# Sparse attention on one core: in each round TensorE turns the last unit's probabilities before it takes the values of the unit three rounds back

## What is computed

```python
s = jnp.einsum('bqgrd,bngd->bgrqn', qb, kc)                    # compressed
p_cmp = jnp.where(vis, jax.nn.softmax(jnp.where(vis, s, NEG)), 0.0)
o_cmp = jnp.einsum('bgrqn,bngd->bqgrd', p_cmp, vc)
...
p_slc = jax.nn.softmax(s, axis=-1)                             # selected
o_slc = jnp.einsum('bgrqkl,bgqkld->bqgrd', p_slc, vg)
...
p_win = jax.nn.softmax(jnp.where(band, s, NEG), axis=-1)       # window
o_win = jnp.einsum('bgrqk,bkgd->bqgrd', p_win, vw)
o = gb[..., 0:1] * o_cmp + gb[..., 1:2] * o_slc + gb[..., 2:3] * o_win
return out @ w_out
```

## Time and profile before

| | |
|---|---|
| median of 3 runs | 1355.41 us (1346.52 to 1356.26) |
| the profiled execution: time, span | 1351.99 us, 1350.0 us |
| mean granted TensorE clock | 0.995 |
| busy: PE, DVE, ACT, POOL | 98%, 68%, 48%, 13% of the span |
| the 24 units in the trace | first score at 375.6 us, last value ends at 446.0 us |

### The profile page before, as it was taken

How to read it: one execution, slowest core, us unless ns; L and a number is a source line. 1 busy time by engine, 2 the same in 40 slices (tenths; PEclk the granted TensorE clock), 3 DMA queues, 4 the chain that set the end, 5 groups by cost and what they waited for, 6 DMA issues and landing times.

```text
span 1350.0 us, 23986 instructions
## 1 busy us (share of the span) xinstructions
PE 1322.0 (98%) x9910; PEld 1192.0 (88%) x9910; DVE 917.4 (68%) x1414; ACT 644.4 (48%) x1122; POOL 170.4 (13%) x130
## 2 busy tenths in 40 slices
PE   8999899999989999999999999999999999999999
PEld 8989899999955999999978777888888888889999
DVE  6976699876878689976634556967543465875554
ACT  6655544444367554455433536332332345555442
POOL 0020112000220011110013000213121001201110
PEclk9999899999989999999999999999999999999999
DMA  8638586666510667655333300455643234414553
GB/s 304 205 125 276 190 281 226 227 228 206 188 42 1 220 234 250 203 186 189 126 117 113 129 32 32 141 168 176 202 142 102 95 99 149 149 63 157 188 188 125
DMA packets 63133, 218.53 MB, mean 162 GB/s; under 512 B 6961, under 2 KB 12977, under 8 KB 60721
## 3 DMA queue, kind: packets, MB, share of 16 engines
q1 hardware_dynamic: 58000, 206.59, 45.8%
q10 hardware_dynamic: 5024, 10.41, 2.1%
HBM read 211.73 MB, written 1.05 MB: 158 GB/s over the span
## 4 chain that ended last, share of the span: by engine, by line
PE 87%; DVE 7%; ACT 3%; DMA 2%; issue 1%; SPq 0%; POOL 0%; ACTq 0%; DVEq 0%; POOLq 0%
PE psum L336 25%; PE psum L337 24%; PE psum L338 24%; PE psum L1277 2%; PE psum L1302 2%; DVE WL L264 2%; PE psum L333 1%; DMA stage<-ab_in 1%; PE psum L335 1%; PE psum L334 1%; PE psum L2740 1%; ACT arena L1402 1%; DVE arena L1360 1%; ACT WH L259 1%; DVE SM L1331 1%
## 5 line engine op out<-in xcount | busy, mean ns | idle before, releaser
L336 PE MATMUL psum<-XX,WH 128*128 128x256 f32 (+1 forms) x1912 | 584.9, 306 | 12.6 <-DVE WL L264 7.9
L337 PE MATMUL psum<-XX,WH 128*128 128x256 f32 (+1 forms) x1912 | 576.8, 302 | 0.0
L338 PE MATMUL psum<-XX,WL 128*128 128x256 f32 (+1 forms) x1912 | 576.7, 302 | 0.0
L264 DVE TENSOR_TENSOR WL<-stage,WH 128x1024 fp32r<-128x1024 f32 x332 | 398.7, 1241 | 210.2 <-ACT WH L259 210.0
L259 ACT ACTIVATE WH<-stage 128x1024 fp32r<-128x1024 f32 x332 | 333.9, 1052 | 324.5 <-PE psum L338 264.1
L336 PEld LDWEIGHTS psum<-XX,WH 128*128 128x128 f32 x1912 | 359.7, 188 | 43.5 <-issue 16.7
L338 PEld LDWEIGHTS psum<-XX,WL 128*128 128x128 f32 x1912 | 360.8, 189 | 15.9
L337 PEld LDWEIGHTS psum<-XX,WH 128*128 128x128 f32 x1912 | 359.7, 188 | 15.6 <-issue 0.5
L2912 POOL TENSOR_TENSOR arena<-arena,con 128x512 f32<-128x512 f32 (+1 forms) x48 | 55.3, 1153 | 372.8 <-DVE con L2827 372.1
L336 PE MATMUL psum<-hidden,WH 128*128 128x256 f32 x352 | 97.5, 277 | 0.0
L338 PE MATMUL psum<-hidden,WL 128*128 128x256 f32 x352 | 97.2, 276 | 0.0
(11 more groups left out here) (291 smaller groups left out, 1786.2 us busy)
## 6 DMA issues: line engine op xcount, KB each, us to landing
stage<-w SPq DMA_DIRECT2D x132, 512.0 KB, 5.1
stage<-merge SPq DMA_DIRECT2D x80, 512.0 KB, 5.1
stage<-in SPq DMA_DIRECT2D x44, 512.0 KB, 4.8
ring<-ada SPq DMA_DIRECT2D x12, 1024.0 KB, 8.6
arena<-ada SPq DMA_DIRECT2D x24, 512.0 KB, 3.6
stage<-ab_in SPq DMA_DIRECT2D x22, 512.0 KB, 6.1
stage<-nsa_in SPq DMA_DIRECT2D x20, 512.0 KB, 5.0
stage<-out SPq DMA_DIRECT2D x16, 512.0 KB, 4.6
```

What stands on the lines that cost most here:

```text
L264: e.tensor_tensor(lo, raw, hi.bitcast(F32), ALU.subtract).then_inc(s_lo, 1)
L336: e.matmul(dst, wh, xh, start=start, stop=False)
L337: e.matmul(dst, wh, xl, start=False, stop=False)
L338: return e.matmul(dst, wl, xh, start=False, stop=stop)
```

## The change

A new argument `turn_first` of `attend_tensor`, set for the `nsa` attention alone, puts value n-3 behind turn n-1 in TensorE's round. No instruction is added or removed, and the other engines' code stays as it is. The change adds lines, so that L1402 is L1404 in the kernel after, L1627 is L1629, and so on; L1277 to L1302 keep their numbers.

```diff
-        def attend_tensor(e, p, units, S, T, scores, values, beside, steps, last=None, behind=iter(())):
+        def attend_tensor(e, p, units, S, T, scores, values, beside, steps, last=None, behind=iter(()), turn_first=False):
...
             for n in range(N + 3):
                 if n + 1 < N:
                     scores(n + 1)
-                if n >= 3:
+                if n >= 3 and not turn_first:
                     values(n - 3, T[(n - 3) % NT])
                 for _ in range(steps[n]):
                     next(beside, None)
                 if N - 1 <= n <= N and last:
                     last(n - N + 1)
                 if 1 <= n <= N:
                     turn(n - 1)
+                if n >= 3 and turn_first:
+                    values(n - 3, T[(n - 3) % NT])
...
-            attend_tensor(e, "n", N.units, N.S, N.T, scores, values, iter(()), N.steps, last)
+            attend_tensor(e, "n", N.units, N.S, N.T, scores, values, iter(()), N.steps, last, turn_first=True)
```

## The result

| | before | change |
|---|---|---|
| median | 1351.79 us (4 runs, 1346.52 to 1356.26) | 1372.62 us (4 runs, 1367.34 to 1373.84) |
| ratio | | 1.0155, 95% interval 1.0127 to 1.0183 |
| the profiled execution: time, span | 1351.99 us, 1350.0 us | 1373.84 us, 1372.0 us |
| mean granted TensorE clock | 0.995 | 0.981 |
| stretch from the first score's start to the last value's end | 70.4 us | 97.3 us |

What follows compares the result with a forecast made beforehand. The prediction took a ring of hand-offs to bound the stretch of the 24 units, with no engine full and turns waiting for VectorE. 1351.99 us plus 14.5 (longer ring) and 7.2 (clock) gave about 1374 us, range 1362 to 1385.

Steps and rivals of the forecast that it cites:

- Turns wait for VectorE; the value was the filling: TensorE's stretch of 24 units: turns 16 and 17 start on VectorE's scale; value 14 filled that wait at no cost.
- Done 1.96 us late in the second half: ScalarE's done waits for the branch-2 value behind the turn; the queue behind it makes turn 17 1.96 us late too.
- Branch 0 at 0.60 us: The branch-0 value now stands between turn 17 and score 20 on TensorE, adding 0.60 us per cycle.
- Branch 1 at nothing: The branch-1 value goes behind a short branch-0 turn; costed at nothing, since nobody needs it before the branch-2 value.
- The sum of the ring, 14.5 us: The hand-offs between engines over the 24 units get longer by 14.5 us in all, or 10.3 if branch-0 values are covered.
- the three cycles of the first half: Cycles of values 2, 5 and 8, each 1.58 us longer, 4.74 us together.
- the middle one: The cycle of value 11, of the first half with its turn in the second: 2.07 us longer.
- the last two with the end: End of the second half: values 17 and 20 at 2.56 us each, value 21 being the last cycle's 0.60.
- The clock, 7.2 us for three falls: TensorE, less busy in the longer stretch, has its clock fall to half three times, costing 7.2 us.
- a fall's full price of 2.4 us: Each fall of TensorE's clock to half loses 2.4 us, if all of it is on the path.
- The total: Whole kernel: 14.5 us and 7.2 us make 21.7 us on the profiled execution's 1351.99 us, so 1373.7 us.
- the rival at 1385.5 us: The clock swings throughout the stretch: 8 falls, 19 us, on top of the 14.5 us; chance 0.13.

Runs made afterwards that it cites:

- the filled change: The change plus products that nobody reads in TensorE's expected waits ahead of scores and turns, which held the clock: 1362.8 us, ratio 1.0075.
- branch 2 alone: The change with only the branch-2 values behind the turn, those of branches 0 and 1 staying ahead: 1363.3 us, ratio 1.0077.
- the kernel with done a round later: The whole change, but done (ScalarE) and finish (VectorE) come one round later in their engines' orders: 1358.8 us, ratio 1.0026.
- the filled kernels: The change and the kernel before, each with products that nobody reads in TensorE's waits: 1362.8 us and 1349.7 us.
- branch 1 alone: The change with only the branch-1 values behind the turn: 1354.4 us, ratio 1.0005.
- branch 0 alone: The change with only the branch-0 values behind the turn: 1356.4 us, ratio 1.0044.
- the two filled versions of before: The kernel before with unread products in TensorE's waits, 1349.7 us; and likewise with VectorE's round as scale, copy, maximum, finish, 1348.5 us.

## Why the prediction was right, and where only a size was off

- **Turns wait for VectorE; the value was the filling.** Shown: at full clock the turns of branches 1 and 2 start on the scale in the kernel before, in the change, and in the filled change.
- **Done 1.96 us late in the second half.** Shown at its place (turn to done 2.13 us, just as forecast, and turn to turn 1.96 us longer) and by branch 2 alone (1.95 us per cycle). That the price is that of the queue behind done, and not of the value, the kernel with done a round later shows.
- **Branch 0 at 0.60 us.** 0.57 by itself; that the two add up, the filled change shows: 11.80 less 9.27 is 2.53, against 1.95 + 0.57 = 2.52.
- **Branch 1 at nothing.** Shown: 9.26 us, ratio 1.0005.
- **The sum of the ring, 14.5 us.** 14.0 us between the filled kernels. Read by scores 6, 12, 15, 18 and 21, the three cycles of the first half take 4.73 us (4.74 forecast), the middle one 2.50 (2.07), the next 2.52 (2.56), and the last two with the end 4.25 (5.12). The middle was too small and the end too large, and the two misses partly cancel.
- **The clock, 7.2 us for three falls.** The mechanism held and the size did not. The profiled execution had six falls, some of them long, 45 us at half clock where three falls of 6.8 us were 20; on the other side a fall's full price of 2.4 us was too high: the one fall of the kernel before cost 1.1 us, and the 45 us of the change cost 14.0, or 0.31 per us against 0.35 in the prediction. Of the two, the count was the larger miss, in this execution. The prediction also added its falls to a time that already held one, so what it has to be set against is 45 - 6.8 = 38 us more at half clock, and 14.0 - 1.1 = 12.9 us. By their mean clocks two of the other three runs of the change had 19 and 22 us less at half clock than the profiled one, that is 16 to 19 us more than the profiled run of before, near the 20 forecast.
- **The total.** 14.5 + 7.2 = 21.7 was forecast; the profiled executions differ by 21.85 us, the medians by 20.8. That it came so near owes something to luck: in the profiled pair the stretch took 14.0 + 12.9 = 26.9 us, and 4.9 us came back for another reason, below. In the medians the parts stand nearer: each against its own set's before, 13.7 us for the order, and 20.8 - 13.7 = 7.1 us for what the clock took beyond its part in before, if the 4.3 us that the filling won there are all clock. These medians carry intervals of some 3 to 4 us to either side, so the agreement to a tenth is chance.

The rule of the Trainium skill that the prediction weighed ("TensorE: Matmul & The Clock Gate", section "A second HAM failure mode: psum-queue depth-cycling": frequent short idling lets the clock swing) describes what the change did: six falls with returns between, after idle times of TensorE no longer than 2.3 us. That it would swing all the way through, the rival at 1385.5 us, is not borne out in the time: 1372.6 us. The profiled execution came near to that rival's count (six falls and 45 us low, where it had eight falls of 6.8 us), but at 14.0 us and not 19.

How the clock chooses its moments is left open. In the kernel with branch 1 alone, whose cycle is that of the kernel before, 17 us were low in the profiled execution against 6.8. That is within what runs of one kernel differ by: the mean clocks of its ten runs lie from 0.990 to 0.996, those of before from 0.990 to 0.995. So a single profile tells little about how often the clock falls.

## What to carry to other kernels

An instruction that stands in an engine's queue ahead of a wait costs nothing as long as that wait ends later anyway; before it is moved behind, look for who consumes its result, and what is queued behind that consumer on the consumer's engine. Here a value of 1.08 us, moved by one place, cost 2 us per cycle through two in-order queues, and not through its own engine. And where a ring of hand-offs gets longer, TensorE gets idler, and its clock can take nearly as much again as the ring (14.0 us beside 14.0 in the profiled execution, 10 to 11 beside 13 to 14 in the medians): a few products that nobody reads, in waits that are there anyway, tell the two costs apart. In the kernel before they won 0.3%.

## What the hardware showed that was not expected

The same products run at two paces at a granted clock of 1.00. These are the windows of 100 us over the same part of the program near the end (line 336 alone: TensorE's busy time, how many, PEclk, DMA share, GB/s), before and then the change:

```profile
1230.00:1330.00 100.00, 79.53 (x284) 1.00 0.55 181
```

```profile
1256.00:1356.00 100.00, 81.18 (x295) 1.00 0.59 190
```

284 against 295 products in the same time, 4%. From one product to the next it is about 0.118 us in the one and 0.113 us in the other, at the same granted clock; the transfers (181 and 190 GB/s) go with the pace. Both paces come in every profiled execution here, not always at the same places. From 160 to 280 us branch 1 alone ran at the slower one and the other eight at the faster; from 1240 to 1320 us before, branch 0 alone and the two filled versions of before ran at the slower one, and the other five at the faster.

That stretch near the end is where the change got back 4.9 us: product for product it is 26.9 us behind until about 1170 us of the kernel before, and 22.1 us at the end. The pace may also be part of why runs of one kernel spread over 12 to 14 us (runs of before with the same mean clock of 0.995 took 1347.3 to 1359.0 us), but with one profile for each kernel no run shows it. What sets the pace, and whether it goes with the order of the instructions, is open.
